# Linear stages of a two-block transformer kernel: PSUM eviction and side steps ahead of the weight split

## What is computed

```python
hn = rmsnorm_2(h, ln_mix[i])
(aq, ak, av, hy, gq, gk, gv, go, glr, gates) = split_cols(hn @ w_in[i], IN_SPLITS)
y_a = attention_mixer(...) @ w_br_attn[i]
y_b = hyena_mixer(...) @ w_br_hyena[i]
y_c = gla_mixer(...) @ w_br_gla[i]
gate = jax.nn.sigmoid(gates.reshape(B, L, N_BRANCH, D_MODEL))
mixed = gate[:, :, 0] * y_a + gate[:, :, 1] * y_b + gate[:, :, 2] * y_c
h = h + mixed @ w_out[i]
h = h + memory_cross_attention(rmsnorm_2(h, ln_x[i]), rmsnorm_2(mem, ln_mem[i]), ...)
hn = rmsnorm_2(h, ln_mlp[i])
h = h + jnp.square(jax.nn.relu(hn @ mlp_w1[i])) @ mlp_w2[i]
```

## Time and profile before

| | us |
|---|---|
| device time, median of three | 3149.94 |
| device time of the profiled execution | 3160.7 |
| span of the profiled execution | 3158.9 |
| TensorE matmul busy | 2904.4 (92%) |
| VectorE busy | 2019.8 (64%) |
| ScalarE busy | 1508.3 (48%) |
| mean granted TensorE clock | 0.938 |

### The profile page before, as it was taken

How to read it: one execution, slowest core, us unless ns; L and a number is a source line. 1 busy time by engine, 2 the same in 40 slices (tenths; PEclk the granted TensorE clock), 3 DMA queues, 4 the chain that set the end, 5 groups by cost and what they waited for, 6 DMA issues and landing times. The chain is left out here.

```text
span 3158.9 us, 44295 instructions
## 1 busy us (share of the span) xinstructions
PE 2904.4 (92%) x18156; PEld 2588.6 (82%) x18161; DVE 2019.8 (64%) x2029; ACT 1508.3 (48%) x1439; POOL 29.1 (1%) x39
## 2 busy tenths in 40 slices
PE   5899998699999999999978798988999898988998
PEld 5699997588888888888863687988899797988998
DVE  5555563588888888888857555555555554555554
ACT  3443443467676776766731326343433236343432
POOL 0000000000000000000000000000000000000000
PEclk7899988699999999999987898999999998999999
DMA  5155540399999999999971232444355342443352
GB/s 166 66 174 187 173 135 14 125 368 336 356 354 336 373 336 348 361 336 356 354 257 54 95 107 90 137 133 134 98 184 186 96 134 81 134 134 120 123 185 93
DMA packets 364951, 618.39 MB, mean 196 GB/s; under 512 B 16664, under 2 KB 201078, under 8 KB 363524
## 3 DMA queue, kind: packets, MB, share of 16 engines
q1 hardware_dynamic: 363644, 610.94, 56.3%
q10 hardware_dynamic: 1162, 5.36, 0.4%
HBM read 611.01 MB, written 5.24 MB: 195 GB/s over the span
## 5 line engine op out<-in xcount | busy, mean ns | idle before, releaser
L350 DVE TENSOR_TENSOR slots_low<-slots,w_hi 128x2048 fp32r<-128x2048 f32 x240 | 541.9, 2261 | 598.0 <-ACT w_hi L339 598.0
L339 ACT ACTIVATE w_hi<-slots 128x2048 fp32r<-128x2048 f32 x240 | 451.1, 1884 | 578.2 <-PE ps L431 280.9
L1182 DVE TENSOR_TENSOR slots_low<-slots,w_hi 128x2048 fp32r<-128x2048 f32 x224 | 504.1, 2286 | 65.2 <-ACT w_hi L1133 65.2
L431 PE MATMUL ps<-x_hi,w_hi 128*128 128x256 f32 x1488 | 442.1, 297 | 81.4 <-DVE slots_low L350 36.4
L431 PE MATMUL ps<-x_lo,w_hi 128*128 128x256 f32 x1488 | 434.0, 292 | 0.0
L431 PE MATMUL ps<-x_hi,slots_low 128*128 128x256 f32 x1488 | 433.4, 291 | 0.0
L1133 ACT ACTIVATE w_hi<-slots 128x2048 fp32r<-128x2048 f32 x224 | 415.9, 1907 | 1.2 <-DMA slots<-in_moe_w_up_dram 1.1
L431 PEld LDWEIGHTS ps<-x_hi,w_hi 128*128 128x128 f32 x1488 | 299.8, 201 | 90.7 <-issue 52.1
L1066 PE MATMUL ps<-slots_low,x_hi 128*128 128x512 f32 x896 | 349.8, 390 | 0.0
L431 PEld LDWEIGHTS ps<-x_lo,w_hi 128*128 128x128 f32 x1488 | 300.0, 202 | 0.5
L431 PEld LDWEIGHTS ps<-x_hi,slots_low 128*128 128x128 f32 x1488 | 298.9, 201 | 0.0
(11 more groups left out here) (527 smaller groups left out, 5616.6 us busy)
## 6 DMA issues: line engine op xcount, KB each, us to landing
slots<-in_moe_w_gate_dram SPq DMA_DIRECT2D x112, 1024.0 KB, 5.1
slots<-in_moe_w_up_dram SPq DMA_DIRECT2D x112, 1024.0 KB, 5.1
slots<-in_moe_w_down_dram SPq DMA_DIRECT2D x112, 1024.0 KB, 4.9
slots<-in_mlp_w_dram SPq DMA_DIRECT2D x64, 1024.0 KB, 5.3
slots<-in_w_in_dram SPq DMA_DIRECT2D x54, 1024.0 KB, 5.3
slots<-in_ffn_w_gate_dram SPq DMA_DIRECT2D x14, 1024.0 KB, 5.0
slots<-in_ffn_w_up_dram SPq DMA_DIRECT2D x14, 1024.0 KB, 5.0
slots<-in_ffn_w_down_dram SPq DMA_DIRECT2D x14, 1024.0 KB, 4.8
```

The source lines that it names most:

```text
L339: act.activation(w_hi[:, s.buffer, 0:s.kt * s.cols], slots[:, s.slot, 0:s.kt * s.cols], ACT.Copy).then_inc(w_hi_done, 1)
L350: dve.tensor_tensor(slots_low[:, s.slot, 0:n], slots[:, s.slot, 0:n], w_hi[:, s.buffer, 0:n].bitcast(F32), ALU.subtract).then_inc(w_lo_don ...
L431: mm = pe.matmul(b[:, t * T:(t + 1) * T], w, xx[:, k, :], **flags)
L1182: dve.tensor_tensor(low[i % NS], raw[i % NS], his[i % R].bitcast(F32), ALU.subtract).then_inc(lo_done, 1)
```

## The change

In both loops the split of slab j + 3 stays at the head of the round up to round nn. In every later round it goes to the end, behind the eviction, the item's own function and the hook. The two splits still wait for the same semaphores.

```diff
@@ -477,7 +477,7 @@
-                        if j < n:
+                        if j <= nn and j < n:
                             split_hi(act, slabs[j].index + NHI - 1)
                         if j == nn:
                             for i, s in enumerate(normed):
@@ -490,6 +490,8 @@
                                 items[j - 1][2](act, more)
                         if ("act", j) in hooks:
                             hooks["act", j](act, more)
+                        if nn < j < n:
+                            split_hi(act, slabs[j].index + NHI - 1)
 
                 @block.vector
@@ -527,6 +529,8 @@
                             empty(dve, "dve", dve_emptied, done)
                         if ("dve", j) in hooks:
                             hooks["dve", j](dve, more)
+                        if nn < j < n:
+                            split_lo(dve, slabs[j].index + NHI - 1)
```

## The result

The changed kernel takes 3098.39 us, the median of six runs (3091.23 to 3100.64), against 3149.91 for the kernel before (six runs, 3144.03 to 3165.41). The ratio is 0.9822, with a 95% interval of 0.9804 to 0.9841: 1.8% faster. The forecast was 3101.3. The profiled execution took 3099.34 us, with a span of 3097.5 and a mean granted clock of 0.949 (0.938 before).

A forecast was written before the change was run, and what follows sets the result against it. TensorE, busy 92% of the span, was taken as the bound, so only its waits and clock count. Over both blocks 35.0 us of waits plus 13.6 of clock make 48.6, from 3149.9 to 3101.3 us; range 3090 to 3127.

The forecast's parts named there:

- cumulate: Branch stage: TensorE's 3.9 us wait for log_decay shrinks to 0.3 to 0.4, so 3.5 us a block goes.
- turn_keys, turn_o, split_o: Branch stage: TensorE's waits of 1.6, 2.0 and 1.7 us behind split pairs all go, 5.3 us a block.
- branch end: Between the branch stage's last slab and the residual stage: last operation 2.5 us earlier, wait 6.0 to 3.5 us, per block.
- norm column, key shift: Memory projections: of TensorE's 4.2 us norm wait 3.9 goes, and all of the 1.3 us key shift wait, per block.
- memory end: Between the memory projections' last slab and the scores: wait 5.0 to 4.0 us, so 1.0 goes per block.
- clock, branch stage: Slow stretches behind the waits for cumulate and turn_o return to full clock, 1.7 us each per block.
- starts of residual and scores: Slow stretches where these stages start: 0.6 us a block regained, since a shortened wait probably keeps most of its slow stretch.
- rival 3: VectorE's side step stands behind the previous round's late split, so each wait only halves: 3126 us, chance 0.11.
- Rival 1: Waits go but TensorE's clock doesn't come back, as slow stretches follow something that remains: 3115 us, chance 0.20.
- rival 4: Nothing moves, because the matmul hooks and not the splits set the waits: 3150 us, chance 0.04.
- Rival 2: Slow stretch behind turn_o's short wait stays, perhaps caused by the following transposes; the longer waits' stretches go: 3105 us, chance 0.15.
- Rival 5: Slower: TensorE starves for the late split where side work now stands ahead of it: 3182 us, chance 0.03.

The follow-up runs named there:

- experiment 5: Changed kernel without the last round's split in the branch stages and latent attention's key stage only; 3092.81 us (ratio 0.9825), measured again at 3090.08 us (0.9796).
- experiment 8: Changed kernel with the split back at the head in round 13 of block one's branch stage and rounds 1 and 2 of block two's; 3103.52 us, ratio 0.9868.
- experiment 7: Changed kernel with the linear stages splitting two slabs ahead instead of three; 3098.4 us, ratio 0.9831.
- kernel 4: Changed kernel, but the last round of each linear stage doesn't split and the next stage catches up; 3103.52 us, ratio 0.9830.

## Why the prediction was right

Its total, 48.6 us, stands against 51.5 in the medians and 50.2 in the stages that the change touches. Waits that stand behind a split went, and the clock behind them came back. Step by step, block one:

| term | forecast | measured |
|---|---|---|
| cumulate | 3.5 of 3.9 goes | 3.7 |
| turn_keys, turn_o, split_o | 5.3 | 5.3, and a 0.3 us wait (L1775) that was not counted |
| branch end | 6.0 to 3.5 | 6.0 to 4.4 |
| norm column, key shift | 3.9 and 1.3 | 3.9 and 1.3 |
| memory end | 5.0 to 4.0 | 5.0 to 3.8 |
| clock, branch stage | 3.4 | 7.0 us at half clock gone: 3.5 |
| clock, behind the norm column | 2.8 | 0.70 to 1.00 over 9.4: 2.8 |
| starts of residual and scores | 0.6 | both blocks -1.3: 0.7 a block |

The measured terms make 14.4 us of the branch stage's 15.1; the other 0.7 I can't place. In the memory projections they make 9.2 of 9.3.

The last line of the table agrees by luck. Block one's two stages are 0.5 us longer together and block two's 1.9 shorter, where the prediction had 0.6 less in each. Its reason, that a shortened wait keeps most of its slow stretch, doesn't describe them: behind the same 4.4 us wait, block one's residual stage has 6.8 us at half clock and block two's 3.4.

*The chain to cumulate* could be followed operation by operation. In the changed kernel the same rounds read, ScalarE first:

```profile
1935.06 0.63 ACT L1613 ACTIVATE share<-share 128x512 f32<-128x512 f32 x1 [1.66 <-DVE share L549]
1936.06 1.08 ACT L1675 ACTIVATE decay_soft<-ps 128x512 f32<-128x512 f32 x2 [0.37 <-PE ps L1669]
...
1940.83 1.06 ACT L1679 ACTIVATE decay_soft<-decay_soft 128x1024 f32<-128x1024 f32 x1
1941.79 1.90 ACT L339 ACTIVATE w_hi<-slots 128x2048 fp32r<-128x2048 f32 x1
```

```profile
1943.72 2.29 DVE L350 TENSOR_TENSOR slots_low<-slots,w_hi 128x2048 fp32r<-128x2048 f32 x1 [5.75 <-ACT w_hi L339]
1945.93 0.68 DVE L549 TENSOR_TENSOR share<-ps,root 128x512 f32<-128x512 f32 x1
1946.53 1.21 DVE L1689 TENSOR_TENSOR decay_soft<-decay_low,decay_soft 128x1024 f32<-128x1024 f32 x1
```

The stage starts 9.6 us earlier in this trace (1924.2 instead of 1933.8). Set back by that, log_decay ends at 1957.3 where the forecast had 1957.6. The 0.3 is for the most part the overlap of operations on one engine, which the forecast's sums left out: behind an eviction of 0.68 the next operation begins 0.60 after its start. This is also the one place inside a stage where a late split stands ahead of a side step that TensorE waits for, the mechanism of rival 3; it costs 0.2 us there.

*The branch end is the step that failed.* The forecast that "slab 16's four operations run as its parts come, the last two by 2071.8 + 1.4 = 2073.2" forgot that the round before now ends with a split too. Its low split held VectorE until 2049.1 (experiment 5's rows), the four operations followed in a row, and the last low split began at 2051.8 rather than behind ScalarE alone. The term is 1.6 and not 2.5, so 1.8 us for both blocks. Rival 3 had the mechanism, a step of round j + 1 behind round j's late split, but gave it to all chains; it holds for this one, whose rounds are full, and by 0.9 us.

*The memory end* was worked out as 3.2 us of work and 0.8 for the barrier. The trace of the changed kernel has 3.27 from the start of the last eviction to the end of the last product, and 0.5 to TensorE's next matmul.

*The rivals.* Rival 1, the clock doesn't come back, is refuted by the 1.00 in the two stretches above and by a branch stage without any half clock, and rival 4 by the result. Rival 2's reason, that the transposes bring the slow stretch, is not borne out: experiment 8 has wait and transposes with the clock at 1.00, in one case. Its outcome didn't come, since the wait itself went. Rival 5 is refuted by experiment 7, with a cover a third smaller.

*What I said of L350's idle time* was wrong, at no cost: it fell from 598 to 405 us. The low split used to be the first thing that VectorE did in a round and waited there for ScalarE's 1.9 us; now the side step fills that time.

*The size.* The median moved by 2.9 us more than forecast, the sum over the stages by 1.6 more; the rest is less than what the clock does in other stages. I had counted both halves of the diff in how much earlier an eviction comes (4.2 us), while VectorE's is enough.

## What to carry to other kernels

Where an engine does both work that the critical engine will want several steps later and work that it wants next, put the latter first; the profile shows beforehand which waits will go, and that a part of the stretch behind each long one runs at half clock, so price both. At a stage's end the same rule asks for the prefetch to be left out where the following stage starts with other work, but not where it starts with the prefetched data: the split left in costs 0.9 us at the branch end, and the split left out costs 4.3 us more waiting at the attention input, 2.7 to 3.1 net of the clock that comes back behind it. Check the edges of a reordering by walking through the last two rounds, not the last alone.

## What the runs showed of the hardware

- The length of an untouched stage differed by 11.7 us between kernels (granted clock 0.62 or 0.93 over the mLSTM heads), with equal work on VectorE; a gain of under 12 us read from one pair of spans could be this alone.
- A wait of 3.9 us cost 5.3 us when it was put back, and one of 2.0 cost 2.2. The clock's share is not in proportion to the wait. Two waits of 2.0 and 2.1 us in one kernel, with the same instructions around them, had 0.82 and 1.00 behind them.
- The residual stage's start ran at 0.62 over 8.0 us behind a 4.4 us wait in block one, and at 0.83 behind the same wait in block two. In kernel 7 it ran at 0.79 behind 4.4 us in block one, and kernel 4 ran at 0.64 there behind 3.5 us. The first two rows are the changed kernel's, block one and two, the third is kernel 4's:

```profile
2058.80:2066.80 8.00, 8.00 (x45) 8.00 (x46) 3.88 (x4) 2.42 (x3) 0.00 (x0) 0.62 0.01 3
2734.45:2742.45 8.00, 8.00 (x57) 8.00 (x57) 4.61 (x5) 3.17 (x4) 0.00 (x0) 0.83 0.01 4
2054.85:2062.85 8.00, 8.00 (x46) 8.00 (x47) 6.12 (x5) 4.25 (x4) 0.00 (x0) 0.64 0.12 42
```

Before the change it was 0.71 behind 6.0 us. How much is lost doesn't follow from the length of the wait alone, and the clock that kernel 5 won in this stretch (0.79 behind 3.5 us in block one) can't be put down to its shorter wait.
